# Hybrid attention layer: the value products of an attention step placed ahead of the weight products and transpositions of the loop turn

## The chip, the cores and the metric

The kernel runs on one core of a Trainium2 chip. The metric is the device time of one execution in microseconds (us). A core has a matrix engine (TensorE, PE in the profile), a vector engine (VectorE, DVE), a scalar engine (ScalarE, ACT), a general engine (GpSimd, POOL) and a queue that issues transfers (SyncE, SP). Each engine works through its own list of instructions in the order in which the program gives them and meets the others at semaphores. TensorE reads SBUF and writes PSUM, which has eight banks of 128 x 512 float32 (`ps[0]` to `ps[7]`, "bank" in the profile); a bank must be copied or consumed by VectorE or ScalarE before it is written anew.

## What is computed

One decoder layer on 512 tokens of width 1024: a feed-forward part, a mixer with two groups of heads side by side, and a second feed-forward part. The change lies in the dilated attention of the mixer:

```
x += 1/2 * SwiGLU_1(RMSNorm(x))
h  = RMSNorm(x);  p = h @ W_in
     GLA head group       (4 heads, chunked gated linear attention)
     attention head group (8 heads of 64, three dilated patterns, rotary on a quarter of each head)
x += W_out @ concat(gla_out, attn_out)
x += 1/2 * SwiGLU_2(RMSNorm(x));  out = RMSNorm_final(x)
```

In each attention head the scores q k' are masked, passed through a softmax over the keys, and multiplied with the values. The three dilated patterns are folded into one mask: a query's weight on a key counts how many patterns see it.

## The kernel before, in words

All weights are split into a rounded part and a remainder (`w_hi` by ScalarE L480, `w_lo` by VectorE L773), and so are the activations, so that each product is three matmuls of 128 x 512 (`product`, L1255 to L1257). Weights come in units of 1 MB through two `raw` buffers. TensorE goes through one written list from the first feed-forward part to the last.

The attention runs in 12 steps: four pairs of heads (`p = s // 3`), and for each pair three groups of query tiles (tile 0 and 1; tile 2; tile 3). The two heads of a pair are `e = 0, 1`. In a step s:

- TensorE `scores(s)` (L1561) writes q k' for both heads to banks 4 and 5: 12 matmuls of 128 columns, 8 of 192, or 8 of 256, by group. It waits until the masks of step s-1 have read these banks.
- VectorE `mask_scores(s)` (L959) adds the mask, writes to SBUF (`probs`) and takes the row's extreme; ScalarE `exp_scores(s)` (L653) takes the exponential; VectorE takes the reciprocal of the sums (L981); the scaling is VectorE's (L988) or ScalarE's (L672).
- TensorE `transpose_probs(s)` (L1577) turns `probs` into banks 2 and 3, one bank a head.
- ScalarE `move_probsT(s)` (L682) copies these banks to SBUF (`probsT`), the head e = 0 first.
- TensorE `weigh_values(s)` (L1594) multiplies `probsT` with the values, 12 or 16 matmuls, into bank 6 or 7. It waits for both copies of its step.

The steps are spread over turns k of a loop on each engine. TensorE's turn k holds the scores of step k, the weight products planned for that turn, the transpositions of step k-2 and the value products of step k-3. The weight products are independent of the attention: halves of the tiles of later head pairs (`project_heads`, 2.7 us each) in turns 0 to 6, and parts of the output product (`gla_part`, L1255 to L1257 on `cat_hi`, `cat_lo`, 1.4 us each) in turns 7, 8 and 10 to 14. `HEAD_STEPS` and `PART_STEPS` name the turns; turn 9 has none. Turns 12 to 14 have no scores.

ScalarE's turn k holds, in this order: the copy of a projected tile (L629, some turns), the exponentials of step k, its share of the scaling of step k-1, `move_probsT(k-2)`, and then, in some turns, the rounding of a weight unit (L480, turns 1 and 4) or of a quarter of one (L662, turns 7 to 10), a rounding of the GLA output (L686) or the square and rounding of a finished pair of heads (L690, L691). VectorE's turn k holds the masks of step k, the scaling of step k-1, the rotary work of a tile (L939, L942, L948, with a product on POOL, L472, between), the remainder of a GLA output (L1066) and, in turns 1 and 4, the remainder of a weight unit (L773).

After the loop TensorE adds the attention's part of the output product (`heads_part`, on `o_hi` and `h_hi`), sums squares (L1655) and goes on to the second feed-forward part.

Of the kernel before, what the change touches and what calls it, by code (L numbers as in the profile page):

```python
# [90 lines left out]
def layer_program(nc, xw_dram, positions, gains_in, up1, down1, w_proj, w_ga, w_v, w_a2, w_o, up2, down2,  # L91
                  const_in, final_gain, out):
    ctx = ExitStack()
    with ctx:
# [243 lines left out]
        def att_values(t, h):  # L338

            return x[:, 2 * t + h // 4, S + HD * (h % 4):S + HD * (h % 4 + 1)]  # L340
# [8 lines left out]
        def strips(s):  # L349

            out, at = [], 0
            for i in ATT_TILES[s % PER_PAIR]:
                out.append((i, slice(at, at + P * (i + 1))))
                at += P * (i + 1)
            return out
# [16 lines left out]
        def unit_size(u):  # L372
            if u >= U_LAST:
                return UP_W
            for base in (0, U_FFN2):
                if base <= u < base + FFN_UNITS:
                    for kind, u0, _, n, a in ffn_phases(base, 0):
                        if u0 <= u < u0 + n:
                            return UP_W if kind == "up" else P * next(b - c for c, b in PARTS if c == a)
            return UP_W  # L380
# [3 lines left out]
        def _(sp):  # L384
# [21 lines left out]
            def ffn(base, up, down):  # L406
                for kind, u0, _, n, a in ffn_phases(base, 0):
                    if kind == "up":
                        phase(u0, n, lambda f: up[f + a])
                    elif u0 == U_LAST:  # L410
                        for v in range(LAST_UNITS):
                            load(u0 + v, 0, down[1][v])
                            if v == 0:
                                sp.dma_start(x[:, 0:4, S:S + 2 * P], final_gain.rearrange("o (a f) -> (o a) f", f=2 * P)
                                             .partition_broadcast(P)).then_inc(gain_landed, 16)
                    else:
                        phase(u0, n, lambda m: down[0 if a == 0 else 1][m])
# [834 lines left out]
        def _(pe):  # L1252
# [224 lines left out]
            def project_heads(n, w, half, chunks=None):  # L1477

                chunks = chunks or range(4 * half, 4 * half + 4)
                if 0 in chunks:  # L1480
                    pe.wait_ge(w_split, U + 9 + n + 1)
                    pe.wait_ge(tile_out, BANK_CREDIT + T + 17 + 2 * (n - 1) + w + 1)
                slot = (U + 9 + n) % 2
                for c in chunks:
                    col = (w * KC + c) * P
                    last = product(ps[w][:], w_hi[slot][:, col:col + P], w_lo[slot][:, col:col + P],
                                   h_hi[:, c, :], h_lo[:, c, :], c == 0, c == KC - 1)
                if KC - 1 in chunks:
                    last.then_inc(tile_done, 1)
# [57 lines left out]
            def scores(s):  # L1547
                p = s // PER_PAIR
                if s % PER_PAIR == 0:
                    pe.wait_ge(rope_done, 2 * p + 2)  # L1550
                if s:
                    pe.wait_ge(s_masked, 2 * s)
                else:
                    pe.wait_ge(gla_half, 2)
                for i, cols in strips(s):
                    pieces = 2 if i else 1
                    width = P * (i + 1) // pieces
                    for c in range(pieces):
                        for e in range(2):
                            r = HD * e  # L1560
                            last = nc.tensor.matmul(ps[4 + e][:, cols.start + c * width:cols.start + (c + 1) * width],  # L1561
                                                    projT[r:r + HD, T_AQ + 2 * p, i * P:(i + 1) * P],
                                                    projT[r:r + HD, T_AK + 2 * p, c * width:(c + 1) * width],
                                                    start=True, stop=True)
                            if i == strips(s)[-1][0] and c == pieces - 1:
                                last.then_inc(s_done, 1)

            def transpose_probs(s):
                for e in range(2):
                    q = 2 * s + e  # L1570
                    pe.wait_ge(act_scaled if on_scalar(s, e) else dve_scaled, scaled_count(s, e))
                    if s:
                        pe.wait_ge(pt_out, q - 1)
                    else:
                        pe.wait_ge(tile_out, BANK_CREDIT + T + 17)
                    for j in range(strip_width(s) // P):
                        last = nc.tensor.transpose(ps[2 + e][:, j * P:(j + 1) * P],  # L1577
                                                   probs[s % PROB_BUFS][e][:, j * P:(j + 1) * P], ident)
                    last.then_inc(pt_done, 1)

            def weigh_values(s):
                p = s // PER_PAIR
                if s % PER_PAIR == 0:
                    if p >= 2:
                        pe.wait_ge(att_ready, p - 1)
                        pe.wait_ge(att_squared, p - 1)
                    else:
                        pe.wait_ge(gla_half, 4)
                pe.wait_ge(pt_out, 2 * s + 2)
                for i, cols in strips(s):  # L1590
                    for j in range(i + 1):
                        for e in range(2):
                            h, at = 2 * p + e, cols.start + j * P
                            last = nc.tensor.matmul(ps[6 + p % 2][HD * e:HD * (e + 1), i * P:(i + 1) * P],  # L1594
                                                    att_values(j, h), probsT[s % 2][e][:, at:at + P],
                                                    start=j == 0, stop=j == i, skip_group_check=True)
                last.then_inc(pv_done, 1)
# [8 lines left out]
            def gla_part(m, half):  # L1606

                if half == 0:
                    pe.wait_ge(w_split, UO + m // 2 + 1)
                    if m < 2:  # L1610
                        pe.wait_ge(tile_out, BANK_CREDIT + T + 23 + m + 1)
                    elif m < 4:
                        pe.wait_ge(s_masked, 2 * ATT_STEPS + m - 3)
                    else:
                        pe.wait_ge(gla_part_out, m - 3)
                for k in (2 * half, 2 * half + 1):
                    if m == 0:
                        pe.wait_ge(cat_ready, k + 1)
                    ins = chunk(m, k, GLA_BANKS[m % 4], cat_hi[:, k, :], cat_lo[:, k, :], k == 0, k == 3)
                if half:  # L1620
                    ins.then_inc(gla_part_done, 1)
# [14 lines left out]
            for k in range(ATT_STEPS + 3):  # L1636
                if k < ATT_STEPS:
                    scores(k)
                for h in range(len(HEAD_STEPS)):
                    if HEAD_STEPS[h] == k:  # L1640
                        project_heads((h + 2) // 4 + 1, (h + 2) % 4 // 2, (h + 2) % 2)
                for h in range(len(PART_STEPS)):
                    if PART_STEPS[h] == k:
                        gla_part(h // 2, h % 2)
                if 2 <= k < ATT_STEPS + 2:
                    transpose_probs(k - 2)
                if k >= 3:
                    weigh_values(k - 3)
            pe.wait_ge(att_squared, 3)
            pe.wait_ge(att_ready, 3)  # L1650
            heads_part(0, (0, 1, 2))
# [130 lines left out]
```

## Time and profile before

| | us |
|---|---|
| median of 3 runs | 964.04 (963.4 to 964.26) |
| the profiled execution, its own time | 963.53 |
| its span, first to last instruction | 961.7 |
| TensorE busy | 952.3 (99%) |
| VectorE busy | 490.2 (51%) |
| ScalarE busy | 338.6 (35%) |

The attention loop takes TensorE from 487.8 to 561.0 us of the span. In a timeline a row is a run of like instructions: its start, how long the run took, and in brackets how long the engine had been idle before it and who released it. A matmul's record ends later than its successor starts, since matmuls overlap: a run of transpositions with 0.81 us holds TensorE for 0.75.

### The profile page before, as it was taken

How to read it: one execution, taken by the hardware profiler on the slowest of the kernel's cores; microseconds unless marked ns; L12 is line 12 of the kernel's file. 1: busy time of each engine (PE TensorE's matmuls, PEld its weight loads, DVE VectorE, ACT ScalarE, POOL GpSimd, SP SyncE). 2: the span in 40 equal slices, each digit the busy share in tenths (PEclk: the TensorE clock that was granted, in tenths of full speed). 3: DMA queues.
4: the chain of work that ended last, by engine and by line, in shares of the span. 5: the costliest groups of instructions: out<-in, count | busy, mean ns of one | idle time of the engine just before them, and what ended most of it. 6: DMA issues, size and time to landing. Idle time of an engine off the chain costs nothing. (4 is left out here: it accounts for less than half of the span.)

```text
span 961.7 us, 12089 instructions
## 1 busy us (share of the span) xinstructions
PE 952.3 (99%) x4714; PEld 775.8 (81%) x4714; DVE 490.2 (51%) x634; ACT 338.6 (35%) x440; POOL 52.3 (5%) x35
## 2 busy tenths in 40 slices
PE   9999999999999999999999999999999999999997
PEld 6888888888888887888778778788888888888885
DVE  6854443335443556554397668744443235644326
ACT  7423221122222335531446963433322112222313
POOL 0870000000000000000022000000000000000000
PEclk9999999999999999999999999999999999999999
DMA  8232222332221233222212012232222332255312
GB/s 323 87 132 87 76 83 92 104 125 88 95 106 55 82 111 119 88 88 91 87 47 86 22 67 88 91 129 87 87 74 90 99 131 88 90 150 153 110 44 88
DMA packets 33187, 94.76 MB, mean 99 GB/s; under 512 B 18560, under 2 KB 19840, under 8 KB 24960
## 3 DMA queue, kind: packets, MB, share of 16 engines
q1 hardware_dynamic: 16080, 91.89, 27.4%
q10 hardware_dynamic: 17072, 2.38, 1.6%
q8 instruction: 24, 0.39, 0.2%
q14 instruction: 11, 0.09, 0.0%
HBM read 90.07 MB, written 2.10 MB: 96 GB/s over the span
## 5 line engine op out<-in xcount | busy, mean ns | idle before, releaser
L1255 PE MATMUL bank<-h_hi,w_hi 128*128 128x512 f32 x824 | 323.5, 393 | 0.0
L1257 PE MATMUL bank<-h_hi,w_lo 128*128 128x512 f32 x824 | 320.7, 389 | 0.0
L1256 PE MATMUL bank<-h_lo,w_hi 128*128 128x512 f32 x824 | 320.7, 389 | 0.0
L480 ACT ACTIVATE w_hi<-raw 128x2048 fp32r<-128x2048 f32 (+2 forms) x87 | 154.7, 1778 | 331.9 <-PE bank L1257 329.8
L773 DVE TENSOR_TENSOR w_lo<-raw,w_hi 128x2048 fp32r<-128x2048 f32 (+2 forms) x87 | 184.6, 2122 | 83.7 <-ACT w_hi L480 83.2
L1255 PEld LDWEIGHTS bank<-h_hi,w_hi 128*128 128x128 f32 x824 | 154.6, 188 | 36.6 <-issue 3.8
L1256 PEld LDWEIGHTS bank<-h_lo,w_hi 128*128 128x128 f32 x824 | 154.7, 188 | 32.3 <-issue 0.7
L1257 PEld LDWEIGHTS bank<-h_hi,w_lo 128*128 128x128 f32 x824 | 154.7, 188 | 32.2
L819 DVE TENSOR_TENSOR prod<-bank,rstd 128x512 f32<-128x512 f32 x44 | 30.4, 690 | 175.9 <-PE bank L1257 175.9
L1255 PE MATMUL bank<-g_hi,w_hi 128*128 128x512 f32 x272 | 105.8, 389 | 0.0
L1256 PE MATMUL bank<-g_lo,w_hi 128*128 128x512 f32 x272 | 105.8, 389 | 0.0
L1257 PE MATMUL bank<-g_hi,w_lo 128*128 128x512 f32 x272 | 105.8, 389 | 0.0
L521 ACT ACTIVATE gate<-gate 128x512 f32<-128x512 f32 x44 | 27.8, 632 | 158.4 <-DVE gate L817 158.4
L835 DVE SCALAR_TENSOR_TENSOR x<-bank,x 128x512 f32 (+1 forms) x24 | 16.6, 692 | 91.0 <-PE bank L1257 91.0
L1255 PEld LDWEIGHTS bank<-g_hi,w_hi 128*128 128x128 f32 x272 | 51.1, 188 | 10.7
L1256 PEld LDWEIGHTS bank<-g_lo,w_hi 128*128 128x128 f32 x272 | 51.1, 188 | 10.6
L1257 PEld LDWEIGHTS bank<-g_hi,w_lo 128*128 128x128 f32 x272 | 51.1, 188 | 10.5
L817 DVE TENSOR_TENSOR gate<-bank,rstd 128x512 f32<-128x512 f32 x44 | 30.2, 685 | 24.9 <-PE bank L1257 22.9
L472 POOL TENSOR_TENSOR projT<-projT,rope_c 128x512 f32<-128x512 f32 x8 | 13.8, 1731 | 455.8 <-DVE square L939 431.3
L828 DVE TENSOR_TENSOR g_lo<-prod,g_hi 128x512 f32 (+1 forms) x44 | 33.4, 760 | 0.7 <-ACT g_hi L525 0.7
L822 DVE TENSOR_TENSOR prod<-prod,gate 128x512 f32<-128x512 f32 x44 | 31.7, 720 | 3.2 <-ACT gate L521 0.6
L1255 PE MATMUL bank<-w_hi,g_hi 128*128 128x512 f32 x80 | 31.1, 389 | 0.0
(217 smaller groups left out, 838.5 us busy)
## 6 DMA issues: line engine op xcount, KB each, us to landing
raw<-in_up SPq DMA_DIRECT2D x43, 1024.0 KB, 4.8
raw<-in_w_proj SPq DMA_DIRECT2D x8, 1024.0 KB, 4.8
raw<-in_down1a SPq DMA_DIRECT2D x8, 768.0 KB, 4.4
raw<-in_down2a SPq DMA_DIRECT2D x8, 768.0 KB, 4.3
raw<-in_down1b SPq DMA_DIRECT2D x8, 640.0 KB, 3.9
raw<-in_down2b SPq DMA_DIRECT2D x5, 1024.0 KB, 4.9
raw<-in_w_v SPq DMA_DIRECT2D x4, 1024.0 KB, 4.8
raw<-in_w_o SPq DMA_DIRECT2D x4, 1024.0 KB, 4.8
```

The lines of the kernel that those rows point to most:

```text
L472: nc.gpsimd.tensor_tensor(projT[:, t, :], projT[:, t, :], rope_c[:], ALU.mult).then_inc(rope_cos, 1)
L480: nc.scalar.activation(w_hi[u % 2][:, 0:size], raw[u % 2][:, 0:size], ACT.Copy).then_inc(w_round, 1)
L521: nc.scalar.activation(gate[:], gate[:], ACT.Silu).then_inc(silu_done, 1)
L773: nc.vector.tensor_tensor(w_lo[u % 2][:, 0:size], raw[u % 2][:, 0:size], w_hi[u % 2][:, 0:size].bitcast(F32), ALU.subtract).then_inc(w_spl ...
L817: nc.vector.tensor_tensor(gate[:], ps[bank][:], rstd[:], ALU.mult).then_inc(tile_out, 1)
L819: nc.vector.tensor_tensor(prod[:], ps[bank + 1][:], rstd[:], ALU.mult).then_inc(tile_out, 1)
L822: nc.vector.tensor_tensor(prod[:], prod[:], gate[:], ALU.mult).then_inc(g_mul, 1)
L828: nc.vector.tensor_tensor(g_lo[:, f, :], prod[:], g_hi[:, f, :].bitcast(F32), ALU.subtract).then_inc(g_ready, 1)
L835: nc.vector.scalar_tensor_tensor(x[:, m, 0:S], ps[4 + j][:], 0.5, x[:, m, 0:S], ALU.mult, ALU.add).then_inc(tile_out, 1)
L1255: nc.tensor.matmul(out, a_hi, b_hi, start=first, stop=False)
L1256: nc.tensor.matmul(out, a_hi, b_lo, start=False, stop=False)
L1257: return nc.tensor.matmul(out, a_lo, b_hi, start=False, stop=last)
```

## The change

On TensorE, `weigh_values(k - 3)` is called behind `scores(k)`, ahead of the turn's weight products and of `transpose_probs(k - 2)`; before, it was called last in the turn. Nothing else is edited: the waits inside the functions, the order on the other engines and every instruction's shape are the same.

```
@@ -1636,6 +1636,8 @@
             for k in range(ATT_STEPS + 3):
                 if k < ATT_STEPS:
                     scores(k)
+                if k >= 3:
+                    weigh_values(k - 3)
                 for h in range(len(HEAD_STEPS)):
                     if HEAD_STEPS[h] == k:
                         project_heads((h + 2) // 4 + 1, (h + 2) % 4 // 2, (h + 2) % 2)
@@ -1644,8 +1646,6 @@
                         gla_part(h // 2, h % 2)
                 if 2 <= k < ATT_STEPS + 2:
                     transpose_probs(k - 2)
-                if k >= 3:
-                    weigh_values(k - 3)
```

On TensorE, turn 3: the end of turn 2's transpositions of step 0 (L1577), the scores of step 3 (L1561) and what follows them (L1594 are the value products of step 0, L1255 and L1256 the turn's weight products):

```order
 L1577 MATMUL bank<-const,probs_1 128x128 x3
 L1561 MATMUL bank<-projT 128x128 x6
+L1594 MATMUL bank<-probsT_0,x 64x128
+L1594 MATMUL bank<-probsT_1,x 64x128
+L1594 MATMUL bank<-probsT_0,x 64x128
+L1594 MATMUL bank<-probsT_1,x 64x128
+L1594 MATMUL bank<-probsT_0,x 64x128
+L1594 MATMUL bank<-probsT_1,x 64x128
 L1255 MATMUL bank<-h_hi,w_hi 128x512
 L1256 MATMUL bank<-h_lo,w_hi 128x512
```

The value products of step 0 now stand one run of scores behind the transpositions of the same step; before, the turn's weight products and the transpositions of step 1 stood between as well.

On TensorE, turn 14, the end of the loop: the last rows of the value products of step 10 are the first two here, then the last weight products on `cat_hi` and the value products of step 11.

```order
 L1594 MATMUL bank<-probsT_0,x 64x128
 L1594 MATMUL bank<-probsT_1,x 64x128
-L1255 MATMUL bank<-cat_hi,w_hi 128x512
-L1256 MATMUL bank<-cat_lo,w_hi 128x512
-L1257 MATMUL bank<-cat_hi,w_lo 128x512
-L1255 MATMUL bank<-cat_hi,w_hi 128x512
-L1256 MATMUL bank<-cat_lo,w_hi 128x512
-L1257 MATMUL bank<-cat_hi,w_lo 128x512
-L1594 MATMUL bank<-probsT_0,x 64x128
-L1594 MATMUL bank<-probsT_1,x 64x128
```

Before, six weight products stood between the turns 13 and 14 of value products; now they stand behind those of step 11, and since turns 12 to 14 have no scores, the value products of steps 9, 10 and 11 follow the transpositions of their own step directly.

## Rows read from the trace of the kernel before

**Rows 1.** The page, part 1, and the core's granted clock: busy us, share, count.
```profile
PE 952.3 (99%) x4714; PEld 775.8 (81%) x4714; DVE 490.2 (51%) x634; ACT 338.6 (35%) x440; POOL 52.3 (5%) x35
...
core 0: 961.7 us, clock 0.998
```

**Rows 2.** Waits of PE, whole span: who for whom, us, times, longest.
```profile
PE bank L1373 <- DVE rope_c L873: 1.5, 1, 1.5
PE bank L1577 <- ACT probsT L682: 0.8, 2, 0.5
PE bank L1307 <- ACT h_hi L492: 0.4, 1, 0.4
PE bank L1561 <- DVE negm L959: 0.2, 1, 0.2
```

**Rows 3.** Timeline of PE, attention loop: start us, us, what, [idle before <-releaser].
```profile
505.48 0.94 PE L1561 MATMUL bank<-projT 64*128 64x128 f32 x12
...
509.95 0.88 PE L1594 MATMUL bank<-probsT,x 128*64 128x128 f32 x12
...
518.95 1.13 PE L1561 MATMUL bank<-projT 64*128 64x256 f32 x8
...
524.67 0.94 PE L1561 MATMUL bank<-projT 64*128 64x128 f32 x12
...
530.21 0.92 PE L1561 MATMUL bank<-projT 64*128 64x192 f32 x8 [0.19 <-DVE negm L959]
531.06 0.50 PE L1255 MATMUL bank<-cat_hi,w_hi 128*128 128x512 f32 x1
...
533.24 1.06 PE L1577 MATMUL bank<-const,probs 128*128 128x128 f32 x8 [0.52 <-ACT probsT L682]
...
540.62 0.89 PE L1577 MATMUL bank<-const,probs 128*128 128x128 f32 x6 [0.31 <-ACT probsT L682]
...
556.60 1.03 PE L1577 MATMUL bank<-const,probs 128*128 128x128 f32 x8
...
559.96 1.09 PE L1594 MATMUL bank<-probsT,x 128*64 128x128 f32 x16
```

**Rows 4.** Timeline of ACT, the same stretch.
```profile
506.40 0.84 ACT L682 ACTIVATE probsT<-bank 128x384 f32<-128x384 f32 x2
...
517.82 1.08 ACT L682 ACTIVATE probsT<-bank 128x512 f32<-128x512 f32 x2 [2.00 <-PE bank L1577]
518.79 1.91 ACT L480 ACTIVATE w_hi<-raw 128x2048 fp32r<-128x2048 f32 x1
...
525.10 0.84 ACT L682 ACTIVATE probsT<-bank 128x384 f32<-128x384 f32 x2
529.63 0.40 ACT L653 ACTIVATE probs<-probs,negm 128x128 f32<-128x128 f32 x1 [3.69 <-DVE negm L959]
...
532.63 0.84 ACT L682 ACTIVATE probsT<-bank 128x384 f32<-128x384 f32 x2
...
557.24 1.08 ACT L682 ACTIVATE probsT<-bank 128x512 f32<-128x512 f32 x2 [2.58 <-PE bank L1577]
```

**Rows 5.** Timeline of DVE, the same stretch.
```profile
520.73 2.29 DVE L773 TENSOR_TENSOR w_lo<-raw,w_hi 128x2048 fp32r<-128x2048 f32 x1 [3.35 <-ACT w_hi L480]
...
523.55 0.69 DVE L959 CUSTOM_DVE_ANT_0 probs<-bank,const 128x512 f32<-128x512 f32 x1
...
528.96 0.28 DVE L959 CUSTOM_DVE_ANT_0 probs<-bank,const 128x128 f32<-128x128 f32 x1
```

**Rows 6.** Busy time by stretch, all engines, turns 8 to 12.
```profile
535.00:554.60 19.60, 19.29 (x166) 14.97 (x165) 12.25 (x38) 19.58 (x51) 1.58 (x1) 1.00 0.15 55
```

**Rows 7.** Timeline of ACT, turns 8 and 9.
```profile
536.99 0.69 ACT L691 ACTIVATE o_hi<-bank,gains 128x512 fp32r<-128x512 f32 x1
537.56 0.73 ACT L653 ACTIVATE probs<-probs,negm 128x512 f32<-128x512 f32 x1
...
538.97 1.13 ACT L672 ACTIVATE probs<-probs,rden 128x384 f32<-128x384 f32 x2
```

More of the change, by code:

```diff
@@ L1638, in _ @@
                     scores(k)
+                if k >= 3:
+                    weigh_values(k - 3)
                 for h in range(len(HEAD_STEPS)):
@@ L1646, in _ @@
                     transpose_probs(k - 2)
-                if k >= 3:
-                    weigh_values(k - 3)
             pe.wait_ge(att_squared, 3)
```

## The prediction

> **What bounds the kernel now.** I read the page's busy shares first: TensorE is busy 99% of the span, and the granted clock is 0.998 of full speed over all of it [rows 1]. The list of its waits comes next: over the whole span it waits 1.5 + 0.8 + 0.4 + 0.2 = 2.9 us, of which 1.9 are the start of the program and 0.8 + 0.2 = 1.0 are in the attention [rows 2]. Behind the attention it waits for nobody. So TensorE's queue is the bound from end to end: whatever idle time a new order puts into it in the attention is passed on in full to the end, and the most that any new order can win here is that 1.0 us. Last I read the timelines of the three engines through the attention loop. Three things are to be seen there. ScalarE copies a step's transposed weights late, well behind the transposition (step 4: 532.63 to 533.47). It is then the one that TensorE waits for, 0.52 and 0.31 us [rows 3, 4]. And in turns 8 to 12 ScalarE is busy for 19.58 of 19.60 us, more than TensorE [rows 6].
>
> **What the change does.** No instruction is added or removed, and the other engines keep their order. The value products of a step hold TensorE for 0.80 us (12 matmuls) or 1.02 (16), the scores for 0.86 or 1.06: some 0.08 less than their rows say (0.88, 1.09, 0.94, 1.13), since the successor starts before the last record ends [rows 3]. What moves is when they are due. Before, between the scores of a turn and the value products stood the turn's weight products and a run of transpositions, 0.75 or 0.97 us; the transpositions needed the copy of the same step anyway, since they write the banks it reads. Now the copies of step k-3 are due as soon as the scores of turn k are through. Everything behind them, the weight products that need no copy included, stands behind the waiting instruction, and the scores of the next turn with them. Those feed the masks, the exponentials and so the next copy, so a delay comes round again. And the transpositions come later in their turn by the 0.8 to 1.0 us of the value products ahead of them, and so do ScalarE's copies where ScalarE waits for them.
>
> The unit of the sums: TensorE resumes 0.14 us after the copy it waits for. The first copy of step 4 begins at 532.63 and lasts 0.47 (0.84 for two, starting 0.37 apart), so it ends at 533.10; the transpositions start at 533.24 [rows 3, 4]. Below, k is a turn; I carry TensorE's delay against its old times, the "lag", along.
>
> 1. k = 3, values of step 0. Scores of step 3 hold TensorE until 505.48 + 0.86 = 506.34. The copies of step 0 run from 506.40 to 507.24 [rows 3, 4]. The products start at 507.24 + 0.14 = 507.38: a wait of 1.05. Lag 1.05.
> 2. k = 4 and 5. the copies of step 1 stand in ScalarE's queue behind the exponentials of step 3, whose scores came ahead of the first wait, so they do not move with the lag, and it covers them: no wait. But the transpositions of step 2 come 0.80 + 1.05 = 1.85 later. ScalarE was already idle for 2.00 us waiting for them, so its copy at 517.82 and the rounding of a weight unit behind it at 518.79 (1.91 us) move by 1.85; VectorE had been idle for 3.35 waiting for that rounding, so its split at 520.73 (2.29) moves too, and behind it the masks of step 5, whose second ends at 523.55 + 0.69 = 524.24 and now at 526.1 [rows 4, 5]. The scores of step 6 wait for these masks: 526.1 + 0.14 against 524.67 + 1.05 = 525.72 [rows 3]. A wait of 0.55. Lag 1.6.
> 3. k = 6, values of step 3. The copies ended at 525.94 (525.10 + 0.84) [rows 4], behind exponentials that waited for the late masks, so they end at 527.8. The scores end 0.86 behind 526.25, at 527.1. A wait of 0.85. Lag 2.45.
> 4. k = 7, values of step 4. The copies ended at 533.47. ScalarE had waited 3.69 us for the masks of step 6, and these (528.96) stood in VectorE's own queue behind the masks of step 5 and a rotation [rows 4, 5], so the whole chain moves by 1.8: copies done at 535.3, products at 535.4. The scores of step 7 were through at 531.06, less the 0.19 that they waited, plus 2.45, come to 533.3 [rows 3]. A wait of 2.1, the largest. The old waits of 0.19 and 0.52 go in return.
> 5. k = 5 and 8: the copies of step 2 are done before the longer scores (1.06 us) and lag 1.05 are over; at k = 8 ScalarE is idle ahead of the transpositions of step 5. No wait.
> 6. k = 9 to 11, the stretch in which ScalarE has no idle time. From the end of a step's scores to the next copies' end runs one chain: first mask 0.7, two exponentials 1.4, scaling 1.0, copies 0.85 with the resume 0.15 [rows 7], some 4.2 us with the hops between engines, and it starts about 0.4 late because the rounding of a pair's output stands before the exponentials (536.99 to 537.56) [rows 7]: 4.6. TensorE has beside it value products 1.02, weight products 1.5, transpositions 0.75, scores 0.86: 4.1. So k = 9 waits 0.5. In turn 9 there are no weight products, and beside the chain of step 9 (4.2 us, with the shared scaling 0.6 in place of 1.0 but a quarter's rounding before it) TensorE has only the end of its own wait, 0.8 + 0.75 + 0.86 = 2.4 us, so k = 10 waits 1.2. k = 11 has 1.06 us of scores and a full turn: none. The old wait of 0.31 goes.
> 7. k = 12 to 14. No scores stand between the transpositions and the value products of the same step. The last step shows it: transpositions start at 556.60, copies at 557.24, 0.64 later, and end at 558.32; with the resume 1.86 us, while the transpositions hold TensorE for 0.97: 0.9. For the 384-column steps 9 and 10 it is 0.6 + 0.84 + 0.14 - 0.75, some 0.85 each [rows 3, 4]. Together 2.6. Before, weight products of 1.4 to 2.7 us hid this. The final products behind it gain slack that they did not lack, under 0.1.
>
> Sum: 1.05 + 0.55 + 0.85 + 2.1 + 0.5 + 1.2 + 2.6 = 8.85, less the 1.0 to 1.1 of waits that go: +7.8 us. The profiled execution of before took 963.53, which makes 971.3; it lay 0.5 under the median, so the median becomes 971.8, 0.8% slower.
>
> The neighbours that no row of before shows (scores directly ahead of value products, value products directly ahead of weight products outside turns 12 to 14) I bound by the joints that are there: a first weight product behind scores has a record of 0.50 us, where that of most is 0.39, so some 0.1 more [rows 3]. The count of changes of kind does not alter, so nothing to plus or minus 0.1 in each of nine turns; I take nothing.
>
> How the rows are read: the transposition at 533.24 stood 0.52 us for a copy though the value products and scores behind it were in the queue, and nothing of them ran in the gap [rows 3]. The Trainium skill (TensorE: Matmul & The Clock Gate, the part on what a matmul computes) says that the engine's reorder window pulls weight loads ahead of running matmuls but leaves the matmuls in program order; were they free to pass each other, the waiting value products would let the weight products by and the sum would be near zero. The trace agrees with the program order.
>
> **Rivals.**
> - *Only the worst wait counts (969.1).* If ScalarE's and VectorE's times did not follow TensorE's, a lag once had would cover the later waits. Then the lag is that of step 4, 533.47 + 0.14 - 531.06 = 2.55, and the three round trips at the end add 2.6: +5.1. For it: the copies of step 1 in item 2 do keep their times. Against it: ScalarE's idle times before 517.82 and 529.63 name TensorE and the masks as releasers [rows 4], so the times do follow.
> - *The other side: no loss or a gain (963.0 to 964.5).* The place is the copy: if every copy of step k-3 ended before the scores of turn k, nothing would wait and the earlier value products would take the transpositions' waits away, at most 1.0 us [rows 2]. It decides at the end of the scores; the copy of step 4 ended 2.4 us behind it in the run of before, and steps 9 to 11 cannot meet it at all. That the compiler undoes the order is excluded by the rows of the order.
> - *The clock falls (about 975).* No row of before has a lower clock in the attention: it is 1.00 in turns 8 to 12 with 0.31 us idle [rows 6]. A wait of 2.1 us is longer than any idle time of TensorE in that trace (1.5 us, at its start [rows 2]). If the clock went to 1.2 GHz for about one turn (3 to 4 us of work from the scores at 530.21 to the transpositions at 533.24 and on), that work would take twice its time: +3.5. The Trainium skill (TensorE: Matmul & The Clock Gate, Part 1) says that the throttled state is the default and that activity releases it; by that rule a stall could cost this on top.
>
> **Numbers.** Forecast 971.8, own range 970 to 973.8, chance 0.73. Only the worst wait (968.5 to 970): 0.13. Clock or more neighbours' cost (974 to 977): 0.09. Other side: 0.05. The range for 8 in 10, with a bit of the rivals on both sides: 969 to 974.6. A change of 0.2% (1.9 us) is what a measurement here tells from none. Slower by more than that 0.95, within 0.04, faster 0.01 (only 1.0 us is there to win).
>
> **What would show it.** In the profile after: TensorE waiting at L1594 for ScalarE's L682 in eight turns of twelve, about 8.3 us in all, longest 2.1 in turn 7; one wait of the scores for the masks of step 5, about 0.5; no wait of L1577 for L682; the last value products starting about 6 us later than 559.96 (they are called one weight product earlier); the clock at 1.00; nothing new behind the loop. Wrong it would be if the list of waits stays near 1 us, if the waits at L1594 sum to much less because ScalarE's copies keep their old times, or if the time goes where TensorE is busy and not where it is idle.

## The result, and the profile after

The changed kernel takes 971.22 us in the median of 6 runs (970.04 to 972.53), the kernel before 964.0 beside it (6 runs, 963.4 to 964.3): ratio 1.0076, 95% interval 1.0066 to 1.0086. It is slower, by 7.2 us where 7.8 were forecast. The profiled execution of after took 970.08 (span 968.3), 6.55 more than that of before.

The waits of TensorE over the whole span (who for whom: us in all, times, longest):

```profile
PE bank L1594 <- ACT probsT L682: 7.4, 8, 2.1
PE bank L1373 <- DVE rope_c L873: 1.5, 1, 1.5
PE bank L1561 <- DVE negm L959: 0.5, 1, 0.5
PE bank L1307 <- ACT h_hi L492: 0.3, 1, 0.3
```

Against [rows 2]: the 0.8 us at the transpositions (L1577) are gone, the value products (L1594), which never waited, wait 8 times for ScalarE's copies, and in place of the 0.2 that turn 7's scores waited for masks, turn 6's wait 0.5. In the attention TensorE stood still for 1.0 us before and stands for 7.9 now: 6.9 more, which is the difference of the spans, 6.6, within the 0.3 by which this execution was already ahead at the start of the affected turns (scores of turn 3 at 505.20 against 505.48 [rows 3]).

The page shows the same in shares: the busy time has not changed, the idle time has.

```profile
PE 952.1 (98%) x4714; PEld 776.1 (80%) x4714; DVE 489.9 (51%) x634; ACT 338.9 (35%) x440; POOL 52.3 (5%) x35
...
core 0: 968.3 us, clock 0.998
```

TensorE's timeline, the rows that answer to [rows 3] and every row that waited:

```profile
505.20 0.94 PE L1561 MATMUL bank<-projT 64*128 64x128 f32 x12
507.11 0.88 PE L1594 MATMUL bank<-probsT,x 128*64 128x128 f32 x12 [0.97 <-ACT probsT L682]
...
525.98 0.94 PE L1561 MATMUL bank<-projT 64*128 64x128 f32 x12 [0.47 <-DVE negm L959]
527.67 0.88 PE L1594 MATMUL bank<-probsT,x 128*64 128x128 f32 x12 [0.75 <-ACT probsT L682]
...
535.07 0.88 PE L1594 MATMUL bank<-probsT,x 128*64 128x128 f32 x12 [2.07 <-ACT probsT L682]
...
537.38 1.03 PE L1577 MATMUL bank<-const,probs 128*128 128x128 f32 x8
538.34 1.13 PE L1561 MATMUL bank<-projT 64*128 64x256 f32 x8
...
543.99 0.88 PE L1594 MATMUL bank<-probsT,x 128*64 128x128 f32 x12 [0.38 <-ACT probsT L682]
...
547.59 0.88 PE L1594 MATMUL bank<-probsT,x 128*64 128x128 f32 x12 [1.07 <-ACT probsT L682]
...
556.01 0.88 PE L1594 MATMUL bank<-probsT,x 128*64 128x128 f32 x12 [0.75 <-ACT probsT L682]
...
559.76 0.88 PE L1594 MATMUL bank<-probsT,x 128*64 128x128 f32 x12 [0.64 <-ACT probsT L682]
...
565.20 1.09 PE L1594 MATMUL bank<-probsT,x 128*64 128x128 f32 x16 [0.74 <-ACT probsT L682]
```

The waits stand in the turns that were named: 3, 6, 7, 9, 10, 12, 13 and 14. In brackets they are counted from the end of the last record, which outlasts the engine's slot by some 0.07 us; from start to start they are 0.05 to 0.08 longer each. The last value products start 5.2 us later than in [rows 3] (565.20 against 559.96), although the six weight products of turn 14, 1.4 us, no longer stand ahead of them.

A measure that starts and ends outside the brackets will be of use for every experiment: the time from the scores of turn 3 to the first product behind the loop, on `o_hi`. Before, it is 560.98 - 505.48 = 55.50 us, after, 567.71 - 505.20 = 62.51: +7.01. The first row is of before, the second of after:

```profile
560.98 0.50 PE L1255 MATMUL bank<-o_hi,w_hi 128*128 128x512 f32 x1
567.71 0.39 PE L1255 MATMUL bank<-o_hi,w_hi 128*128 128x512 f32 x1
```

It leaves out what varies ahead of the affected turns. The scores of turn 3 start anywhere from 504.73 (e1) to 506.06 (e12) in the profiles of this case, although nothing in TensorE's list ahead of them was changed. Below it is called the loop time.

The delay travelling through ScalarE and VectorE, against [rows 4] and [rows 5]. ScalarE first:

```profile
506.12 0.84 ACT L682 ACTIVATE probsT<-bank 128x384 f32<-128x384 f32 x2
...
519.40 1.09 ACT L682 ACTIVATE probsT<-bank 128x512 f32<-128x512 f32 x2 [3.62 <-PE bank L1577]
520.37 1.92 ACT L480 ACTIVATE w_hi<-raw 128x2048 fp32r<-128x2048 f32 x1
...
526.68 0.84 ACT L682 ACTIVATE probsT<-bank 128x384 f32<-128x384 f32 x2
...
534.18 0.84 ACT L682 ACTIVATE probsT<-bank 128x384 f32<-128x384 f32 x2
```

And VectorE:

```profile
522.32 2.29 DVE L773 TENSOR_TENSOR w_lo<-raw,w_hi 128x2048 fp32r<-128x2048 f32 x1 [4.64 <-ACT w_hi L480]
...
525.14 0.69 DVE L959 CUSTOM_DVE_ANT_0 probs<-bank,const 128x512 f32<-128x512 f32 x1
...
530.52 0.28 DVE L959 CUSTOM_DVE_ANT_0 probs<-bank,const 128x128 f32<-128x128 f32 x1
```

The copies of step 2 come 1.58 us later than before, the rounding behind them too, the split 1.59, the masks of step 5 1.59, those of step 6 1.56, the copies of step 4 1.55. The copies of step 0 keep their place against the rest (506.12 against 506.40 less the 0.28 of head start). Since this execution was 0.28 ahead, the shifts of 1.55 to 1.59 are delays of 1.83 to 1.87 by the order, where the prediction had 1.85.

What this profile does not show is why the six times spread over 2.5 us, in two groups (970.0 to 970.7, 971.8 to 972.5), where those of before spread over 0.9. That became the question of the last experiments.

### The profile page after: what moved, and what is told of

It is laid out like the page before. It is cut to its first block, busy times and chain, and to the rows that moved or that the text cites. A ratio compares the mean times of both kernels' runs of the same rounds, so it can differ in the third digit from the quotient of the medians.

```text
span 968.3 us, 12089 instructions
## 1 busy us (share of the span) xinstructions
PE 952.1 (98%) x4714; PEld 776.1 (80%) x4714; DVE 489.9 (51%) x634; ACT 338.9 (35%) x440; POOL 52.3 (5%) x35
## 4 chain that ended last, share of the span: by engine, by line
PE 93%; ACT 3%; DVE 2%; issue 2%; DMA 1%; POOL 0%; SPq 0%; DVEq 0%; ACTq 0%; POOLq 0%
PE bank L1255 30%; PE bank L1257 29%; PE bank L1256 29%; ACT probs L653 1%; PE bank L1594 1%; ACT probsT L682 1%; DMA x<-in_xw 1%; ACT probs L672 0%; DVE probs L959 0%; PE bank L1315 0%; PE bank L1317 0%; PE bank L1307 0%; PE bank L1577 0%; PE bank L1272 0%; PE bank L1561 0%
## 5 line engine op out<-in xcount | busy, mean ns | idle before, releaser
L1255 PE MATMUL bank<-h_hi,w_hi 128*128 128x512 f32 x824 | 323.4, 392 | 0.0
L1257 PE MATMUL bank<-h_hi,w_lo 128*128 128x512 f32 x824 | 320.8, 389 | 0.0
L1256 PE MATMUL bank<-h_lo,w_hi 128*128 128x512 f32 x824 | 320.7, 389 | 0.0
L1255 PEld LDWEIGHTS bank<-h_hi,w_hi 128*128 128x128 f32 x824 | 154.6, 188 | 35.9 <-issue 4.0
L1256 PEld LDWEIGHTS bank<-h_lo,w_hi 128*128 128x128 f32 x824 | 154.7, 188 | 32.5 <-issue 0.7
L1257 PEld LDWEIGHTS bank<-h_hi,w_lo 128*128 128x128 f32 x824 | 154.6, 188 | 32.3
L1255 PE MATMUL bank<-g_hi,w_hi 128*128 128x512 f32 x272 | 105.8, 389 | 0.0
L1256 PE MATMUL bank<-g_lo,w_hi 128*128 128x512 f32 x272 | 105.8, 389 | 0.0
L1257 PE MATMUL bank<-g_hi,w_lo 128*128 128x512 f32 x272 | 105.8, 389 | 0.0
L1256 PEld LDWEIGHTS bank<-g_lo,w_hi 128*128 128x128 f32 x272 | 51.1, 188 | 10.7
L1257 PEld LDWEIGHTS bank<-g_hi,w_lo 128*128 128x128 f32 x272 | 51.1, 188 | 10.6
L1255 PEld LDWEIGHTS bank<-g_hi,w_hi 128*128 128x128 f32 x272 | 51.1, 188 | 10.5
L1255 PE MATMUL bank<-w_hi,g_hi 128*128 128x512 f32 x80 | 31.1, 389 | 0.0
```

Of the source, the lines that this page charges most:

```text
L1255: nc.tensor.matmul(out, a_hi, b_hi, start=first, stop=False)
L1256: nc.tensor.matmul(out, a_hi, b_lo, start=False, stop=False)
L1257: return nc.tensor.matmul(out, a_lo, b_hi, start=False, stop=last)
```

## The experiments

Each was timed over 5 rounds beside the kernel before. "Theory" is the prediction's: the products wait because the time that covered the copies is gone, and the wait runs through TensorE's one queue.

**e1, only turns 12 to 14 moved.**

```
+                if k >= 3 and k >= 12:
+                    weigh_values(k - 3)
...
+                if k >= 3 and not (k >= 12):
                     weigh_values(k - 3)
```

> The value products are moved ahead of the weight products only in turns 12 to 14. Theory (a move costs the cover between transposition and value products, and the round trip to ScalarE then lies bare): in turn 12 the copies of step 9 are late by 1.5 to 1.7 us, turns 13 and 14 wait 0.8 each, +3.2 to 3.4 us over before; three waits at L1594 for L682, and the old 0.5 and 0.3 at L1577 stay. Rival (each moved run costs the same, by its new neighbours: 7.2 us for 12 runs, 0.6 a run): +1.8 us with no waits at L1594 to match.

Measured: 966.28 us against 963.24, ratio 1.0031 (1.0019 to 1.0043), +3.0. The profile has three waits at L1594 and both old ones:

```profile
551.49 0.88 PE L1594 MATMUL bank<-probsT,x 128*64 128x128 f32 x12 [1.47 <-ACT probsT L682]
...
555.25 0.88 PE L1594 MATMUL bank<-probsT,x 128*64 128x128 f32 x12 [0.64 <-ACT probsT L682]
...
560.69 1.09 PE L1594 MATMUL bank<-probsT,x 128*64 128x128 f32 x16 [0.74 <-ACT probsT L682]
```

They sum to 2.85, and the loop time grows by 2.97, which is the loss. A price per moved run is out: it would give 1.8 and no waits.

**e2, only turn 7 moved** (the same edit with `k == 7`).

> The value products are moved only in turn 7. Theory: TensorE waits at L1594 for the copies of step 4, 2.4 us, and wins back the 0.5 of the same turn's transpositions and some 0.3 of turn 9's: +1.6 us. Rival (same cost for each moved run): +0.6. Rival (delays add up and come round again by themselves): +2.4 or more.

Measured: 965.89 against 963.24, ratio 1.0027 (1.0016 to 1.0038), +2.65. In the profiled execution (965.06, +1.8) there is one wait at L1594 of 2.39 us and the old waits at L1577 are gone, as the theory has it: a wait that comes earlier takes the later ones' place. The price per run is out. The loop time grows by 1.44, near the theory's 1.6. But the median is 1 us above the theory. Four of the seven executions, 965.89 to 966.51, have a mean clock of 0.996 to 0.997, the other three, 965.1 to 965.5, have 0.998; the kernel before never had less than 0.998 in the runs beside it. The profiled execution is one of the three.

**e3, behind the weight products, ahead of the transpositions.**

```
+                if k >= 3:
+                    weigh_values(k - 3)
                 if 2 <= k < ATT_STEPS + 2:
                     transpose_probs(k - 2)
-                if k >= 3:
-                    weigh_values(k - 3)
```

> In every turn the value products stand behind the weight products and ahead of the transpositions. Theory (the weight products are the cover): nearly all of the loss goes; the transpositions still come 0.8 to 1.0 us later, which delays a copy, a weight unit's split and two masks: +1.2 us over before (waits: S of step 6 0.6, S of step 7 0.5, value products of step 4 1.0, of step 6 0.5, old transposition waits gone). Rival (late transpositions are what costs): +5 to +7, as in the change.

Measured: 964.74 against 963.24, ratio 1.0015 (1.0006 to 1.0024), +1.5. The waits at L1594 are two, 1.0 us in all (theory: two, 1.5), and the scores wait twice for masks, 0.7 (theory 1.1). So the loss goes down from 7 us to 1.5, and the theory had 1.2: of the two runs that the value products were moved past, the weight products were the cover. The waits do not explain all of the 1.5, though. The profile's loop time grows by 1.53. From start to start TensorE's waits in it are 1.98 us against 1.35 before, 0.6 more. The other 0.9 stands in no wait. Turn 3, which has none, shows it:

```profile
509.09 0.88 PE L1594 MATMUL bank<-probsT,x 128*64 128x128 f32 x12
509.89 0.88 PE L1577 MATMUL bank<-const,probs 128*128 128x128 f32 x6
510.70 0.92 PE L1561 MATMUL bank<-projT 64*128 64x192 f32 x8
```

From the scores of turn 3 to those of turn 4 it takes 510.70 - 505.27 = 5.43 us, before 510.75 - 505.48 = 5.27. Between value products and scores the transpositions hold TensorE for 0.81 us, where they held it for 0.75, and the value products begin 0.32 us behind the start of the last weight product (508.77), where the transpositions began 0.23 behind it. In this order the neighbours cost 0.16 us in this turn; in the changed order they do not, as e4 and the loop time of the changed kernel show.

**e4, in the changed place, one turn later.**

```
                 if k < ATT_STEPS:
                     scores(k)
+                if k >= 4:
+                    weigh_values(k - 4)
```

(the loop has one more turn, and the old call is gone)

> The value products stand where the change put them, directly behind the scores, but those of step k-4, so each runs one turn later and just behind the next scores. Theory (what costs is that the copy has had no time, not the place): +0 to +0.5 us over before, no waits at L1594. Rival (the place behind the scores or ahead of the weight products costs by itself): +5 to +7.

Measured: 963.53 against 963.24, ratio 1.0005 (0.9996 to 1.0014), no difference. No wait at L1594; three for masks, 1.1 us, and one of 0.2 at the transpositions. The products stand exactly where the change put them, behind the scores and ahead of the weight products, and cost nothing that the times tell (the loop time grows by 0.33, the waits by 0.3). What the change took away is time, not a good neighbour.

**e5, the changed kernel with VectorE's split behind the masks.**

```
                 if k < ATT_STEPS:
                     mask_scores(k)
+                if k == 5:
+                    split_next(U + 11, 0)
...
-                if k in (1, 4):
-                    split_next(U + 10 + (1, 4).index(k), 0)
+                if k == 1:
+                    split_next(U + 10, 0)
```

> The changed kernel, with VectorE's split of the weight unit of turn 4 moved behind the masks of step 5. Theory (the delay of the transpositions of step 2 goes through ScalarE's rounding and this split into the masks and from there into three waits): the wait of the scores of step 6 (0.5) and that of the value products of step 3 (0.8) go, that of step 4 stays at 2.1 to 2.4; 1.2 us under the changed kernel, +5.9 over before. Rival (waits are independent): only the 0.5 goes.

Measured: 970.69 against 963.72, ratio 1.0072 (1.0058 to 1.0086): +7.0, no better than the changed kernel, where theory and rival had both expected a gain. Yet the waits did what the theory says: the scores' wait and that of turn 6 are gone, turn 7's is 2.22, and TensorE's waits in the attention sum to 6.8 where the changed kernel has 7.9. The time went elsewhere. All five executions have a mean clock of 0.996 or 0.997. The timeline behind turn 7's wait (L1596 is the value products' line here, L1257 to L1259 the weight products'):

```profile
534.17 1.29 PE L1596 MATMUL bank<-probsT,x 128*64 128x128 f32 x12 [2.22 <-ACT probsT L682]
535.40 0.79 PE L1257 MATMUL bank<-cat_hi,w_hi 128*128 128x512 f32 x1
535.99 0.63 PE L1258 MATMUL bank<-cat_lo,w_hi 128*128 128x512 f32 x1
536.41 0.63 PE L1259 MATMUL bank<-cat_hi,w_lo 128*128 128x512 f32 x1
...
539.00 1.14 PE L1563 MATMUL bank<-projT 64*128 64x256 f32 x8
```

And the same stretch by windows (us, PE busy and count, granted clock, DMA share, GB/s):

```profile
532.00:534.00 2.00, 0.00 (x0) 1.00 0.00 0
534.00:536.00 2.00, 1.82 (x14) 0.62 0.00 0
536.00:538.00 2.00, 2.00 (x6) 0.52 0.00 0
538.00:540.00 2.00, 2.00 (x17) 1.00 0.00 0
```

After the wait the granted clock falls to half, 1.2 GHz, and the matmuls follow each other at 0.42 us instead of 0.23. From the value products to the next scores it takes 539.00 - 534.17 = 4.83 us; in the changed kernel's profile, without the fall, 538.34 - 535.07 = 3.27. The fall costs 1.56 us. This is the prediction's third rival, seen at work. For the mean clock over the span it is (1 - 0.62) x 2 + (1 - 0.52) x 2 = 1.72 us lost, 0.0018 of 969.

**e6 and e7, slower copies in the changed kernel and in the one before.**

```
+                    for part in (2 * q, 2 * q + 1):
+                        nc.scalar.activation(wa2[:, 5 * part:5 * part + 5], ones[:, 0:5], ACT.Copy)
                     nc.scalar.activation(probsT[s % 2][e][:, 0:width], ps[2 + e][:, 0:width], ACT.Copy).then_inc(pt_out, 1)
```

> The changed kernel, with two 5-column ScalarE operations on a free tile ahead of each of the 24 copies, some 0.4 us a copy, 0.8 a step. Theory (the copies are due at once in every turn): every turn pays all of the 0.8, +8 to +9 us over the changed kernel, 16 over before. Rival (only the worst waits set the end): +3 over the changed kernel.

> The kernel before with the same two small operations ahead of each copy. Theory (weight products and transpositions cover the copies, save in turns 7 to 12 where ScalarE has no idle time): +4.5 to +5.5 us over before, little over half of what the same operations cost the changed kernel. Rival (the order of TensorE does not alter what a slower copy costs): as much as the other kernel pays, +8 to +9.

Measured: e6 975.01, e7 966.50, both against 963.72: ratios 1.0115 (1.01 to 1.0131) and 1.0028 (1.0019 to 1.0038). Both numbers were expected too high, since the two operations take 0.19 us ahead of a copy and not 0.4:

```profile
535.50 0.29 ACT L683 ACTIVATE wa<-const 128x5 f32<-128x5 f32 x2
535.69 0.47 ACT L684 ACTIVATE probsT<-bank 128x384 f32<-128x384 f32 x1
```

So a step pays 0.38, the 12 steps 4.6 us. The changed kernel lost 4.1 or 4.2 of them (11.3 over before, where it has itself 7.2 and, in e9, 7.1), nearly all; the kernel before lost 2.8, 0.6 of them. The theory's "every turn pays all" is right for the most part only. The order decides how much of a copy's length counts. The comparison is coarse: e6's profile also has the fall of the clock (0.50 from 538 to 540 us), and which other executions have it is not known. By the profiles it comes out alike: the loop time grows by 12.50 in e6 and by 7.01 in the changed kernel, which with 1.5 for the fall leaves 4.0 for the copies, and by 2.46 in e7.

**e8, the kernel before with what was learned.** e5's edit, and the weight products of turn 10 in turn 9, which had none: `PART_STEPS = (7, 8, 9, 11, 12, 13, 13, 14)`.

> The kernel before, with the split behind the masks of step 5 and the weight products of turn 10 moved to turn 9, which had none. Theory (what is left to win in the attention is the 1.0 us of TensorE's waits): -0.7 to -0.9 us. Rival (ScalarE, without idle time in turns 8 to 12, keeps the pace): 0 to -0.4.

Measured: 962.62 against 963.72, ratio 0.9986 (0.9977 to 0.9995), -1.1 us. It beats both kernels. One wait of 0.15 us is left in the attention (0.2 in the list):

```profile
PE bank L1375 <- DVE rope_c L873: 1.5, 1, 1.5
PE bank L1579 <- ACT probsT L682: 0.2, 1, 0.2
```

**e9, the changed kernel again** (no edit).

> The changed kernel once more, for its spread: its six times lay in two groups, 970.0 to 970.7 and 971.8 to 972.5, where those of before lie within 0.9. Theory (behind the 2.1 us wait of turn 7 the clock falls to 1.2 GHz in some executions, as in the profile of e5, 1.5 to 1.8 us): two groups again, the slower one with a mean clock 0.001 to 0.002 lower. Rival (the chips or sessions differ): one group, with the clock as in the kernel before of the same session.

Measured: 970.57 against 963.5, ratio 1.0078 (1.0064 to 1.0092); five times, 969.74 to 970.57 and 971.97, 972.16. The two groups are there again, on one chip. The lower clock expected of the slower one is not: all five print 0.998. A fall takes 0.0018 off the mean (e5), and wherever its presence is known the mean is 0.996 or 0.997 (the profiled executions of e5, e6 and e12). What moves the third digit otherwise is the end of the span, where TensorE has nothing left to do and the clock goes down too, in one kernel earlier than in another. First the kernel before (0.998), then e3 (0.999, the shortest such end of all the profiles):

```profile
956.00:958.00 2.00, 0.00 (x0) 0.83 0.27 104
958.00:960.00 2.00, 0.00 (x0) 0.50 0.44 157
...
958.00:960.00 2.00, 0.00 (x0) 1.00 0.34 131
960.00:962.00 2.00, 0.00 (x0) 0.92 0.75 261
962.00:963.00 1.00, 0.00 (x0) 0.50 0.01 3
```

With e3's end, 0.66 us lost or 0.0007, a fall could just print 0.998, with any longer one 0.997 or less. Of the five slower executions of the changed kernel here and in the first measurement four print 0.998, and only the slowest, 972.53, has 0.996. So the printed clock speaks for a fall in that one and against it in the four; what makes these slower is open. The profile of e9 has the first group's time, the 2.06 us wait and a clock of 1.00 behind it.

**e10, every turn but 7 moved** (e1's edit with `k != 7`).

> The value products are moved in every turn but 7, so that no wait is longer than about 1.1 us. Theory: +5.5 to +6.1 us over before, in one group, the clock never under 0.998; the wait of turn 7 is worth little by itself, since the others come in its place, but the fall of the clock goes. Rival (the clock falls for the sum of the waits, or at random): the same spread and low clocks as the changed kernel.

Measured: 968.64 against 963.5, ratio 1.0054 (1.004 to 1.0068), +5.1; five times within 0.85, clocks 0.998 and 0.999. Longest wait 1.01 us. One group and no low clock, with waits of 5.5 + 0.5 us still: this agrees with the long wait, not the sum, being what lets the clock fall. Five executions do not prove it, since the changed kernel itself printed a low clock in only one of eleven. The loss is 0.4 us under the expected range; the profile's loop time, +5.55, is inside it. That range still had the waits of turns 12 to 14 at 2.6, and they are 2.12 here as in the changed kernel.

**e11, e5's wait filled with work.**

```
+                if k == 7:
+                    pe.wait_ge(tile_out, BANK_CREDIT + T + 24)
+                    for _ in range(2):
+                        nc.tensor.matmul(ps[0][:], ones, const[:, C_TRI:C_TRI + S], start=True, stop=True)
                 if k >= 3:
                     weigh_values(k - 3)
```

> Kernel e5, whose clock fell in all five executions, with two matmuls of 128x512 float32 on a free bank ahead of the value products of turn 7, 1.7 us of work inside the 2.2 us wait; their result is overwritten. Theory (TensorE standing still is what lets the clock fall): the wait shrinks to 0.5, nothing comes later, the clock is 0.998 and the time 1.5 us lower than e5's, +5.4 over before. Rival (the 1.5 us of e5 have another cause): as e5, +7.0, or more by the added matmuls.

Measured: 969.35 against 963.5, ratio 1.0059 (1.0045 to 1.0073), five times 968.98 to 969.49, clocks 0.998 and 0.999. That is 1.34 us under e5, by adding matmuls that nobody needs, put at 1.7 us and in the profile 1.99 (the two appear as four records):

```profile
531.96 1.99 PE L1644 MATMUL bank<-const 128*128 128x512 f32 x4
534.26 0.88 PE L1596 MATMUL bank<-probsT,x 128*64 128x128 f32 x12 [0.31 <-ACT probsT L682]
```

The value products start at the same time as in e5 (534.26, 534.17), since they wait for the same copy, but their run lasts 0.88 us and not 1.29. The loop time grows by 5.85, in e5 by 7.40: 1.55 us between them, the price of the fall once more. The idle time itself, not its cause, brought the clock down. The mean clocks say the same of all executions: 0.996 or 0.997 in the five of e5, 0.998 or 0.999 in the five of e11.

**e12, only turns 3 to 11 moved** (e1's edit with `k < 12`).

> The counterpart of e1: the value products are moved in turns 3 to 11 only. Theory: five waits at L1594 as in the changed kernel and the 0.5 of the scores, the old waits gone: +4.5 to +5 us over before, +6.2 to +6.7 in executions whose clock falls behind turn 7. Rival (the parts add up: changed kernel less e1): 7.2 - 3.0 = +4.2.

Measured: 968.32 against 963.5, ratio 1.0051 (1.0037 to 1.0064). Five times: 967.75, 967.94, 968.32 with clock 0.999, and 969.86, 970.31 with 0.996 and 0.997. Here the two groups and the two clocks go together, 1.5 to 2.6 us apart; against before they are +4.2 to +4.8 and +6.4 to +6.8. What lies above 1.5 in the distance need not be the clock: the scores of turn 3 start at 506.06 in the profile, 0.86 later than in the changed kernel's. Its profile is of the slower group and has the changed kernel's 2.06 us wait, with the fall behind it:

```profile
535.94 0.95 PE L1594 MATMUL bank<-probsT,x 128*64 128x128 f32 x12 [2.06 <-ACT probsT L682]
536.82 0.79 PE L1255 MATMUL bank<-cat_hi,w_hi 128*128 128x512 f32 x1
537.41 0.63 PE L1256 MATMUL bank<-cat_lo,w_hi 128*128 128x512 f32 x1
...
540.75 1.13 PE L1561 MATMUL bank<-projT 64*128 64x256 f32 x8
```

540.75 - 535.94 = 4.81 us against the 3.27 without a fall: 1.54. So one and the same wait is followed by a fall in this execution and by none in the changed kernel's. The median of the three executions without a low clock, +4.4, does not tell the theory's +4.5 from the rival's +4.2. The loop times do: 6.19 less 1.54 is 4.65 here, where the changed kernel's less e1's is 7.01 - 2.97 = 4.04. The parts do not add up, since e1 pays 1.47 for turn 12 and the changed kernel 0.75.

The loop time of each profiled execution, over that of before (55.50 us), beside the medians, over before in the same session:

| | loop time | median | fall of the clock in the profile |
|---|---|---|---|
| changed kernel | +7.01 | +7.2 | no |
| e9, the same again | +7.01 | +7.1 | no |
| e1, turns 12 to 14 | +2.97 | +3.0 | no |
| e2, turn 7 | +1.44 | +2.65 | no |
| e3, ahead of the transpositions | +1.53 | +1.5 | no |
| e4, one turn later | +0.33 | +0.3 | no |
| e5, split behind masks | +7.40 | +7.0 | yes |
| e10, all but turn 7 | +5.55 | +5.1 | no |
| e11, e5 filled | +5.85 | +5.85 | no |
| e12, turns 3 to 11 | +6.19 | +4.8 | yes |

## Why the prediction was right, and where it was not

The mechanism stands, step by step.

- *TensorE's queue is the bound and passes idle time on in full.* Right: 6.9 us more of waits, 7.01 more of loop time, 6.6 more of span with 0.28 of head start, nothing new behind the loop.
- *Item 1, 1.05 us.* 507.11 - 505.20 - 0.86 = 1.05. Right.
- *Item 2, no wait in turns 4 and 5, then 0.55 through rounding, split and masks.* Right: with the head start counted the engines moved by 1.83 to 1.87 us, and the wait is 0.54 from start to start. e5 removed it by taking the split out of the chain.
- *Items 3 and 4, 0.85 and 2.1.* 0.83 and 2.14 from start to start. e2 shows that a lone turn 7 gives the wait 2.4 and takes the old ones away.
- *Item 6, 0.5 and 1.2.* 0.46 and 1.14 (brackets 0.38 and 1.07).
- *Item 7, 2.6.* The brackets say 0.75 + 0.64 + 0.74 = 2.13, start to start 0.82 + 0.70 + 0.81 = 2.33. This is the term of the sum that was mis-sized most, 0.27 too large, in all three turns. e1 gives these turns alone 3.0 us, because turn 12's wait is 1.47 there: without the earlier waits ScalarE has not caught up.
- *Less the waits that go, 1.0 to 1.1.* The brackets say 1.0, start to start 1.35 (0.27 + 0.69 + 0.39). The new waits were counted from start to start and the old ones by their brackets, which overstated the net by some 0.3 more.

So the new waits are 8.49 us from start to start where 8.85 were forecast, and the net is 7.1 where 7.8 was. The profiled execution, the lowest but one of six, lies at +6.55, and the lower group of the changed kernel's times in e9 (969.74 to 970.57) at +6.2 to +7.1. The median of 971.22 lies between the two groups, and that it came within 0.6 us of the forecast is in part luck: the net was taken 0.7 too large, and what makes the slower group slower was not in the sum.

That the neighbours cost nothing is borne out for the changed order: the waits give 7.14 from start to start, the loop time 7.01. It would not have held for the order of e3.

The rivals. *Only the worst wait counts* is out: e10 without the worst wait still loses 5.1. *The other side* is out. *The clock falls* was held apart as an unlikely case at +3.5 us. It is a thing that comes and goes between executions of the same kernel (e12): profiled in e5, e6 and e12, absent in the profiles of the changed kernel, e2, e9, e10 and e11, and priced at 1.54 and 1.56 us where it was profiled. In e2 the executions with and without a low mean clock are 0.4 to 1.5 us apart. The prediction said 3.5, doubling a whole turn's work; in e5 the clock was back within 4 us of the value products' start, and half of the work that fitted in between is what was lost. The Trainium skill (TensorE: Matmul & The Clock Gate, Part 1) says that the throttled state is the default and that activity releases it; e5 and e11, with the same wait once empty and once filled, agree. That the slower group of the changed kernel itself has the fall is not shown: none of its slower executions was profiled. The groups of e12 and e10's single group speak for it, the printed clock, 0.998 in four of its five executions, against it. The cause of that group stays open.

## What to carry to other kernels

When the bound engine works through one queue, an operation that waits for another engine's answer needs independent work between the request and itself; count that work in microseconds against the answer's round trip, and place the waiting operation last (or, as in e4, a turn later) before looking at anything else. Sum the waits of the profile against the difference of the spans: if they do not match, look at the granted clock behind the longest wait, as in e5, and then at the time that runs take in turns without a wait, as in e3. A wait of some 2 us on TensorE can cost 1.5 us more than itself, in some executions and not in others. Its sign is a mean clock lower by 0.002; a spread of the times alone can have other causes.

## What the runs showed of the hardware

- The granted clock fell from 2.4 to 1.2 GHz behind idle times of 2.02 (e6), 2.06 (e12) and 2.22 us (e5) and stayed at 1.00 behind waits of 2.06 and 2.07 (e9, the changed kernel) and 2.39 us (e2). The length of the idle time alone does not decide. Behind waits up to 1.5 us no fall was seen in the profiles. What else decides was not tried.
- Two matmuls of 128x512 float32 put into a 2.2 us wait made the kernel 1.34 us faster (e11 against e5, 1.55 by the loop times).
- The same transpositions hold TensorE for 0.81 us between value products and scores (e3) and for 0.75 between weight products and value products (before).
- A ScalarE operation on 5 columns has a record of some 0.2 us, but two of them hold the engine for 0.19 together (e6).
